# Splitting the low-part subtraction of every weight tile between VectorE and GpSimd

## The reference

```python
for l in range(2):                      # first block
    proj = rmsnorm(x) @ w_in[l]         # 1024 x 3404
    mix  = four kinds of attention over 256 tokens (one picks its keys by a top-64)
    x    = x + rmsnorm(mix @ w_out[l])
    x    = x + rmsnorm(square(relu(rmsnorm(x) @ w_mlp_up[l])) @ w_mlp_down[l])
    x    = x + sigmoid(x @ w_ple_gate[l]) * (p[l] @ w_ple_proj[l])
for l in range(2):                      # second block
    mix  = concat(gmlp gate, gated delta rule, dilated attention)(x @ w_in_2[l]) @ w_out_2[l]
    x    = layer_norm(a * x + mix)
    x    = layer_norm(a * x + (swiglu if l == 0 else moe_swiglu)(x))
```

## Time and profile before

| | |
|---|---|
| median of 3 runs | 2234.4 us (2233.55 to 2235.82) |
| profiled execution: its own time | 2234.4 us |
| profiled execution: span from first to last instruction | 2232.5 us |
| PE busy | 2105.9 us, 94% of the span |
| DVE busy | 1600.8 us, 72% |
| ACT busy | 1241.6 us, 56% |
| POOL busy | 126.9 us, 6% |
| mean granted TensorE clock | 0.964 of 2.4 GHz |

### The profile page before, as it was taken

One profiled execution on the slowest core, in us unless ns is written; L12 is line 12 of the kernel. 1 busy time (PEld: TensorE's weight loads), 2 busy tenths in 40 slices (PEclk: granted clock), 3 DMA queues, 4 the chain that ended last, 5 costly groups with the idle time before them and its releaser, 6 DMA issues.

```text
span 2232.5 us, 28576 instructions
## 1 busy us (share of the span) xinstructions
PE 2105.9 (94%) x10772; PEld 1787.3 (80%) x10772; DVE 1600.8 (72%) x1589; ACT 1241.6 (56%) x1322; POOL 126.9 (6%) x178
## 2 busy tenths in 40 slices
PE   7979999998999999889998988899999999999995
PEld 5867888786788888878888887788888888888884
DVE  6755654775565478675548866889898988989896
ACT  5544444554444456334434632677777777777772
POOL 0301000030100000210000020000000000000000
PEclk9979999997999999999999998999999999999997
DMA  8404555540455554036545403699999999999993
GB/s 285 130 23 164 172 187 186 191 139 28 157 178 183 190 197 134 19 99 192 186 168 189 133 1 123 232 338 358 345 357 340 353 344 358 338 341 362 345 358 112
DMA packets 152618, 476.32 MB, mean 213 GB/s; under 512 B 14440, under 2 KB 41552, under 8 KB 152400
## 3 DMA queue, kind: packets, MB, share of 16 engines
q1 hardware_dynamic: 149904, 465.65, 59.0%
q0 software_dynamic: 2624, 9.44, 1.2%
HBM read 474.00 MB, written 1.05 MB: 213 GB/s over the span
## 4 chain that ended last, share of the span: by engine, by line
PE 83%; DVE 9%; ACT 4%; DMA 2%; issue 1%; POOL 1%; SPq 0%; DVEq 0%; POOLq 0%; ACTq 0%
PE G L600 19%; PE G L602 19%; PE G L601 19%; PE Sp L600 4%; PE Sp L602 4%; PE Sp L601 4%; PE G L626 3%; DVE ring_lo L1825 2%; PE G L1275 2%; DMA ring<-in_w_in 1%; ACT ring_hi L1380 1%; PE G L1303 1%; ACT ARENA L1464 1%; PE G L909 1%; PE Sp L1166 1%
## 5 line engine op out<-in xcount | busy, mean ns | idle before, releaser
L2483 DVE TENSOR_TENSOR e_lo<-e_raw,e_hi 128x1408 fp32r<-128x1408 f32 x384 | 600.9, 1620 | 24.8 <-ACT e_hi L1760 22.9
L1760 ACT ACTIVATE e_hi<-e_raw 128x1408 fp32r<-128x1408 f32 x384 | 521.0, 1380 | 159.4 <-DMA e_raw<-in_moe_w_down 56.6
L1825 DVE TENSOR_TENSOR ring_lo<-ring,ring_hi 128x2048 fp32r<-128x2048 f32 (+2 forms) x179 | 402.0, 2256 | 222.4 <-ACT ring_hi L1380 220.8
L1380 ACT ACTIVATE ring_hi<-ring 128x2048 fp32r<-128x2048 f32 (+2 forms) x179 | 336.4, 1885 | 244.7 <-PE G L602 193.0
L600 PE MATMUL G<-ring_hi,xTh 128*128 128x512 f32 (+2 forms) x912 | 362.8, 398 | 24.2 <-DVE ring_lo L1825 13.8
L602 PE MATMUL G<-ring_hi,xTl 128*128 128x512 f32 (+2 forms) x912 | 354.5, 389 | 0.0
L601 PE MATMUL G<-ring_lo,xTh 128*128 128x512 f32 (+2 forms) x912 | 354.0, 388 | 0.0
L600 PE MATMUL G<-e_hi,xgTh 128*128 128x512 f32 (+1 forms) x768 | 290.0, 378 | 4.2 <-DVE e_lo L2483 4.2
L602 PE MATMUL G<-e_hi,xgTl 128*128 128x512 f32 (+1 forms) x768 | 289.1, 376 | 0.0
L601 PE MATMUL G<-e_lo,xgTh 128*128 128x512 f32 (+1 forms) x768 | 287.1, 374 | 0.0
L600 PEld LDWEIGHTS G<-ring_hi,xTh 128*128 128x128 f32 x912 | 173.6, 190 | 64.7 <-issue 19.2
(11 more groups left out here) (393 smaller groups left out, 2996.7 us busy)
## 6 DMA issues: line engine op xcount, KB each, us to landing
e_raw<-in_moe_w_gate SPq DMA_DIRECT2D x128, 704.0 KB, 5.9
e_raw<-in_moe_w_up SPq DMA_DIRECT2D x128, 704.0 KB, 6.0
e_raw<-in_moe_w_down SPq DMA_DIRECT2D x128, 704.0 KB, 5.8
ring<-in_w_in SPq DMA_DIRECT2D x48, 1024.0 KB, 5.1
ring<-in_w_mlp_up SPq DMA_DIRECT2D x32, 1024.0 KB, 5.3
ring<-in_w_mlp_down SPq DMA_DIRECT2D x32, 1024.0 KB, 4.8
ring<-in_w_out SPq DMA_DIRECT2D x16, 1024.0 KB, 4.9
ring<-in_ffn_w_gate SPq DMA_DIRECT2D x22, 512.0 KB, 3.9
```

The lines of the kernel that those rows point to most:

```text
L1380: nc.scalar.activation(ring_hi[:, n % H, 0:m], ring[:, n % R, 0:m], ACT.Copy).then_inc(w_hi.sem, 1)
L1760: nc.scalar.activation(e_hi[:, u, :], e_raw[:, u, :], ACT.Copy).then_inc(w_hi.sem, 1)
L1825: v.tensor_tensor(ring_lo[:, n % R, cs], ring[:, n % R, cs], ring_hi[:, n % H, cs].bitcast(F32), ALU.subtract).then_inc(w_lo.sem, 1)
L2483: v.tensor_tensor(e_lo[:, u, :], e_raw[:, u, :], e_hi[:, u, :].bitcast(F32), ALU.subtract).then_inc(w_lo.sem, 1)
```

## The change

The low part of a tile is split by columns. DVE makes the first 11/16 (1408 of 2048 columns, 912 of 1328, 726 of 1056) and raises `w_lo`; POOL makes the rest (640, 416, 330) with the same subtraction and raises a semaphore of its own, `w_lo_pool`. PE waits for both. Thirty-two tiles stay whole on DVE (`whole_dve`: 14 to 21, 50 to 58, 69 to 76 and 105 to 111); the other 147 are split. POOL gets a `met` of its own that, unlike those of the other engines, is called at few places, often for a whole stage at once: before `rms` and the rotations for the tiles of `w_in`, before the last `rms` for those of both MLP products, and in the second block before the level masks (tiles up to 123 or 174), between the gates' scaling and the wait for `o_ms` (three tiles: 124 to 126, and 175 to 177), and between the roots of block 0 and block 1 of `post_norm` (two tiles) and behind them (two more, or one).

```diff
--- before.py
+++ after.py
@@ -340,7 +340,7 @@
     misc_loaded = sig("misc_loaded")
     misc_used = sig("misc_used")
     w_in_slot = [Signal(ctx.enter_context(nc.semaphore(f"w_in_slot{i}"))) for i in range(R)]
-    w_hi, w_lo = sig("w_high_part"), sig("w_low_part")
+    w_hi, w_lo, w_lo_pool = sig("w_high_part"), sig("w_low_part"), sig("w_low_part_pool")
     w_used = sig("w_used")
     g_half = sig("g_first_half")
     x_full = [sig("x_full0"), sig("x_full1")]
@@ -429,15 +429,22 @@
 
 
     TILES = []
+    whole_dve = []
     for l in range(DEPTH):
+        if l:
+            whole_dve += range(len(TILES), len(TILES) + LEAD)
         for pieces in IN_CHUNKS:
             TILES += uses_pieces(w["w_in"][l], pieces)
+        whole_dve += range(len(TILES), len(TILES) + LEAD)
         rows = uses_rows(w["w_out"][l])
         TILES += rows[2:] + rows[:2]
+        whole_dve += range(len(TILES), len(TILES) + LEAD)
         for n0 in range(0, D_FF, 512):
             TILES += uses_cols(w["w_mlp_up"][l], n0, n0 + 512)
         TILES += uses_rows(w["w_mlp_down"][l])
+        whole_dve += range(len(TILES), len(TILES) + 1 + LEAD)
         TILES += uses_rows(w["w_ple_proj"][l]) + uses_rows(w["w_ple_gate"][l])
+    whole_dve += range(len(TILES), len(TILES) + 2)
     for l in range(DEPTH):
         for i in SEQ2:
             TILES += uses_cols(w["w_in_2"][l], *IN2_CHUNKS[i])
@@ -451,6 +458,15 @@
     def floats_of(use):
 
         return sum(m * D if c0 is None else 4 * m for _, c0, m in use)
+
+    def of_dve(n):
+
+        m = floats_of(TILES[n])
+        return m if n in whole_dve else m * 11 // 32 * 2
+
+    def pool_parts(n):
+
+        return n - sum(t < n for t in whole_dve)
 
     def slot_cols_of(buf, slot, width):
         return buf[:, slot, 0:4 * width].rearrange("p (k n) -> p k n", k=4)
@@ -593,6 +609,7 @@
             n = n_use["pe"]
             n_use["pe"] += 1
             pe.wait_ge(w_lo.sem, n + 1)
+            pe.wait_ge(w_lo_pool.sem, pool_parts(n + 1))
             return n % H, n % R
 
         def product(out, ah, al, bh, bl, start, stop, **kw):
@@ -1821,7 +1838,7 @@
                 n = n_lo[0]
                 n_lo[0] += 1
                 dve.wait_ge(w_hi.sem, n + 1)
-                cs = slice(0, floats_of(TILES[n]))
+                cs = slice(0, of_dve(n))
                 v.tensor_tensor(ring_lo[:, n % R, cs], ring[:, n % R, cs], ring_hi[:, n % H, cs].bitcast(F32), ALU.subtract).then_inc(w_lo.sem, 1)
 
         def met(n, ahead=H - 1):
@@ -2571,6 +2588,20 @@
             pool.wait_ge(s_in.sem, s_in.next("pool"))
             power(dst, src, n, s_out)
 
+        n_lo = [0, 0]
+
+        def met(n, ahead=H - 1):
+
+            n_lo[1] += n
+            while n_lo[0] < min(n_lo[1] + ahead, U0):
+                t = n_lo[0]
+                n_lo[0] += 1
+                if t in whole_dve:
+                    continue
+                cs = slice(of_dve(t), floats_of(TILES[t]))
+                pool.wait_ge(w_hi.sem, t + 1)
+                g.tensor_tensor(ring_lo[:, t % R, cs], ring[:, t % R, cs], ring_hi[:, t % H, cs].bitcast(F32), ALU.subtract).then_inc(w_lo_pool.sem, 1)
+
         def rope(x, cos, sin, heads, width, a, b, s=None):
 
             xv = x.rearrange("p (h d) -> p h d", h=heads)
@@ -2593,6 +2624,7 @@
         pool.wait_ge(c_loaded[0].sem, 16)
         gains_loaded(1)
         rms()
+        met(1)
         gains(0, "norm_post_mix", 0)
         for l in range(DEPTH):
             if l:
@@ -2600,7 +2632,9 @@
                 rms()
 
                 gains(0, "norm_post_mix", l)
-
+                met(1)
+
+            met(2 * IN_N - 1, 0)
 
             def rotated(col, heads, width, tb, s=None):
                 cos, sin = (RCOS32, RSIN32) if width == 32 else (RCOS, RSIN)
@@ -2632,26 +2666,32 @@
                 asked(r8[:, 4 * tb:4 * tb + 4], ms8[:, 4 * tb:4 * tb + 4], 4)
             for q in range(2):
                 gains_loaded(q)
+            met(4, 0)
             rms_behind_rms()
+            met(0)
 
             gains(0, "norm_post_mlp", l)
             load(PLE, w["p"][l, 0].rearrange("(t p) d -> p t d", p=P), misc_loaded)
             gains_loaded(0)
+            met(32, 0)
             rms()
 
             gains(1, *(("norm_pre_mix", l + 1) if l + 1 < DEPTH else ("ln1_b_2", 0)))
             if l == DEPTH - 1:
                 load(WSA, w["a_ws_2"][0].rearrange("g t s -> t g s"), misc_loaded)
+            met(5, 0)
         for l in range(DEPTH):
             if l:
 
                 pool.wait_ge(d2pe.sem, vec_free[2 * l - 1])
                 gains(0, "ln1_g_2", l)
                 gains(1, "ln1_b_2", l)
+            met(2)
             layer_norm()
             if l == 0:
 
                 gains(0, "ln1_g_2", 0)
+            met(2 * len(IN2_CHUNKS) - 2, 0)
 
             pool.wait_ge(d2p.sem, d2p.next("pool"))
             for lv in range(1, LEVELS):
@@ -2673,7 +2714,9 @@
                 power(r8[:, cs], ms8[:, cs], 4, o_root)
             for q in range(2):
                 gains_loaded(q)
-            layer_norm()
+            met(4, 0)
+            layer_norm(between=lambda: met(0, 2))
+            met(0, LEAD)
             if l + 1 < DEPTH:
                 load(WSA, w["a_ws_2"][l + 1].rearrange("g t s -> t g s"), misc_loaded)
 
@@ -2683,7 +2726,9 @@
             for q in range(2):
                 gains_loaded(q)
             if l == 0:
-                layer_norm()
+                met(2 * NCH2 + FT2 // 2, 0)
+                layer_norm(between=lambda: met(0, 2))
+                met(0)
 
         layer_norm(f_r, f_p)
 
```

## The result

The kernel after the change takes 2261.6 us (median of 4 runs, 2257.4 to 2264.5) against 2234.0 us for the kernel before (2232.7 to 2235.8): ratio 1.0121, 95% interval 1.0100 to 1.0143. It is slower by 27.6 us. The forecast was 2250 us, slower by 15.9, with a range up to 2258: the direction is right, the size is not. The profiled execution took 2264.95 us itself, 30.5 more than the one of before.

The account below looks back on a forecast made before the run. PE, busy for 94% of the span, was taken to bound the kernel, with `ring_lo` 2% of the chain. Terms 3.7 - 1.0 + 1.0 + 3.0 + 5.6 + 2.2 + 1.4 = 15.9 us on 2234.4 gave 2250 us, range 2235 to 2258.

Parts of the forecast that it names:

- Taking turns: DVE and POOL alternate whole instructions on SBUF; a split tile costs busy DVE about 0.8 us more, not 0.67 less.
- First columns: Layer 0, PE's wait for the copy of `COLS`: turns with pieces of tiles 4 to 8, +3.7 us (-0.9 to +4.6).
- Last columns: End of `w_in`, twice: POOL's rotations start later and DVE's L1987 gets free, -0.5 us a layer, -1.0.
- End of the first block: First piece of tiles 112 to 114 falls into the sum into x before PE's transposes, +1.0 us.
- Columns of `w_in_2`: Twice: some seven split tiles meet convolution instructions, delaying PE's wait at 872.83; +1.5 us each, 3.0.
- States: Delta rule, twice: POOL's piece queued ahead of the root delays state step 3, +2.8 us each, 5.6.
- Second root: Behind it, l = 0: pieces of tiles 130 and 131 take two turns from DVE, +2.2 us (-0.7 to +2.6).
- Down product: Behind it, l = 0: the piece of tile 163 goes ahead of L2184, one turn, +1.4 us (0 to +1.5).
- TensorE's second wait: PE's added wait instruction for each tile: costed at nothing; otherwise a gap would show at each tile.
- more than I count: Rival: pieces nearer 1.6 us and turns delaying ACT in attention; upper bounds 23.6 us, 2258 us or beyond; chance 0.08.
- No turns: Rival: piece and low part don't alternate, only the late root costs; 2236 us, within 0.2%; chance 0.13.
- my signs: PE's waits grow: `COLS` 0.86 to above 4 us, 872.83 to near 4, 998.42 above 8, 1191.80 above 7.

Follow-up runs that it names:

- run 1: Against the changed kernel, GpSimd's piece is a memset to zero that reads nothing (its columns' low part left out): 2230.9 us, 0.9985 of the kernel before.
- Run 2: Against the changed kernel, GpSimd's piece is a multiplication by zero reading one operand (low part left out): 2237.7 us, 1.0016 of the kernel before.
- run 3: Against the changed kernel, GpSimd's share is one eighth of a tile (256 of 2048 columns) instead of five sixteenths: 2244.6 us, 1.0044 of the kernel before.
- run 6: Against the changed kernel, only the `w_in` tiles stay split, with the first four tiles whole on VectorE: 2241.8 us, 1.0038 of the kernel before.
- run 5: Against the changed kernel, only `w_in_2` tiles stay split, with 117 to 120 and 168 to 171 whole on VectorE: 2236.8 us, 1.0014 of the kernel before.
- Run 7: Against the changed kernel, GpSimd's piece behind the delta rule's z product comes after the first root instead of ahead of both: 2256.3 us, 1.0103 of before.
- run 8: Against the changed kernel, only MLP, down, gate and up tiles stay split, and TensorE waits only where a piece exists: 2235.6 us, 1.0003 of before.
- second execution: The changed kernel itself, unaltered, in a later profiled execution: 2258.05 us.

## Why the forecast was right in direction and short in size

**Taking turns** was right, and is now shown by runs 1 to 3 and not by analogy, for pieces that read. The Trainium skill (SBUF — State Buffer, section Who interferes with whom) has GpSimd's reads of SBUF and a DVE instruction of two SBUF inputs exclude each other for whole instructions; runs 1 and 3 agree. Run 2 does so only for GpSimd, which waits 1.4 us: DVE lost at most 0.55 us to a one-operand piece of 1.81 us, and there the measurement decides. My size for the piece, 1.45 us, was low: undisturbed it takes 1.53 to 1.57 us, yet adds at most 1.40 us to DVE.

1. *First columns*: forecast +3.7, measured +5.2 to +5.5, and 1.5 to 1.6 more behind them by the clock, which I had not counted. The mechanism is right; I costed tiles 0 to 3 at nothing, and of the delay at `COLS` they are 1.7 us (run 6), though later stages take most of that back.
2. *Last columns*: forecast -1.0, measured -1.4 to -1.5, at PE's waits for ACT at 101.63 (1.54 us before, 0.26 after) and 493.33 (0.89 before, 0.26 after). DVE's L1987 gets free in layer 0, from 0.93 to 0.35 us; that this is what shortens the wait is not shown. In layer 1 it had nothing to win, and I had misread: both its rows have a rotation of POOL beside them. In layer 1 POOL paid, with 0.90 us instead of 0.73:

```profile
81.33 0.73 POOL L2579 TENSOR_TENSOR XN<-ARENA,ROT 128x256 f32<-128x256 f32 x1 [69.19 <-ACT ARENA L1485]
...
473.68 0.90 POOL L2579 TENSOR_TENSOR XN<-ARENA,ROT 128x256 f32<-128x256 f32 x1 [57.17 <-ACT ARENA L1485]
```

3. *End of the first block*: +1.0 against +0.9. Right.
4. *Columns of `w_in_2`*: +3.0 against +6.8 to +6.9. **This is the step that failed.** I counted seven late low parts, took DVE's idle time off and looked for the loss at 872.83. The loss is earlier, at TensorE's sum of squares, which needs the XN that ends the convolution and had 0.4 us of slack (XN ready at 848.38 + 1.51 = 849.89, TensorE at 850.33). The rows of DVE and PE before:

```profile
848.38 1.51 DVE L2284 SCALAR_TENSOR_TENSOR XN<-Sp,COLS,ARENA 128x128 f32<-128x128 f32 x4
...
850.33 1.88 PE L1096 MATMUL Sp<-ARENA,C 128*128 128x512 f32 x4
```

And it is not made by low parts: run 5 shows that it is POOL's pieces of four tiles, released by ACT's high part 5 to 10 us before DVE's own order comes to them, that lengthen the convolution, three by 1.2 us each and the fourth by 0.6. What the two waits for XN cost is then 3.6 and 2.7 us, and 1.8 and 3.1 us more by the clock behind them, a term that I had put at nothing. Some comes back further on, at the waits for GL and by the clock.
5. *States*: +5.6 against +5.7 in both executions. Place, order of the queue and size right, and run 1 bears it out: a memset in the same place, which takes no turns, makes the states late by 0.9 us less in each layer and is 0.9 us shorter. Run 7 adds that removing the late root gives only 3.2 of the 5.7 us back, as the pieces then fall on DVE.
6. *Second root*: +2.2 against +1.7.
7. *Down product*: +1.4 against +1.3 to +1.6. Right.

Beside the clock behind the waits, two terms were missing. **TensorE's second wait** was costed at nothing; it is nothing in each tile, but 1.2 to 2.2 us behind the experts' loop (run 8), where I had said that both traces are alike. **The clock**: the stretch at 1.2 GHz between 174 and 192 us makes 5.5 us of the profiled execution, and a like difference ahead of it 1.6. By their times, 5 of 11 executions of the changed kernel are in the upper group, 3 of 10 of the run with the waits alone and 12 of 88 of the kernel before; the stretch itself can be seen only in the profiled ones. Whether the change makes it more frequent stays open. The table's last column does not have it; I put the distance from its 23.6 us to the 27.6 us of the medians down to how the executions of both kernels fall into the two groups, which is argued and not shown.

The second execution adds up: forecast 15.9, step 1 +1.5, behind it +1.6, step 2 -0.4, step 4 +3.8, step 5 +0.1, the loop's end +2.3, the others -1.2 together, is 23.6 us.

Of the rivals, "more than I count" came out, but with its surplus behind step 1 and at step 4, at places that it did not name. "No turns" falls with runs 1 and 3. Of my signs, PE's wait for `COLS` grew to 3.3 us and not above 4, the ones at 998.42 and 1191.80 grew to 7.97 and 6.51 us and not above 8 and 7, and the one at 872.83 shrank, from 2.19 to 1.60 us, as the delay had been taken in front of it.

## What to carry to other kernels

Work given to a second engine that shares the first one's way to memory is not taken off it: price each piece at what it adds to the first engine's instructions (here up to 1.4 us for 0.67 us saved), and try the same piece as a memset, which shows in one run what the placement and the shorter parts would give without the turns. A helper engine without an order of its own runs ahead and pushes its work in front of more urgent work; look for the wait with the least slack near each place where it is released, also where no row of idle time stands yet. Where TensorE is the bound, read its granted clock behind each new wait: here the wait was up to half of its price. And an instruction that costs nothing where it stands can cost where an engine leaves a loop, so wait only for parts that exist.

## What was not expected of the hardware

- A GpSimd instruction that reads one SBUF operand waits for nearly the whole of DVE's two-operand instruction (3.25 us against 1.81, beside 1.62) but adds only 0.55 us to it; with two operands of the same 640 columns it adds 1.40 us. A memset of 640 columns (0.64 us) neither waits nor delays.
- What GpSimd's two-operand subtraction adds to DVE is in proportion to its columns: 0.57 us for 256, 1.40 us for 640.
- Behind idle times of 3.3, 3.6 and 2.7 us TensorE ran at 1.2 GHz for a few us (granted 0.56, 0.68 and 0.56), which cost 1.5, 1.8 and 3.1 us beyond the wait; behind three others, twice 2.8 and once 3.2 us, it was granted 1.00.
- Three convolution instructions of DVE, one SBUF operand times a column plus another, 1.52 us, take 2.72 us beside one piece: 1.2 us, less than the 1.4 us of a low part.
- 179 added waits on TensorE cost nothing in the tiles where they are always met, and 1.2 to 2.2 us behind the loop; with 85 or 110 the wait there is 2.5 us, as before.
